# Attention B of a hybrid trunk layer: results of blocks 1 to 3 kept as [d, rows], in place of a turn back and a second transpose

## What is computed

```python
def _mixer_b(q, k, v, q_idx, k_idx, w_idx, rel_bias_b):     # 8 heads of 64, one shared k and v
    def block(args):                                         # 128 queries at a time
        ...
        _, idx = lax.top_k(score, n_sel)                     # 256 of the admissible keys
        ...
        logits = jnp.einsum('bqhd,bqkd->bqhk', qb, k_sel).astype(jnp.float32) * (B_HEAD_DIM ** -0.5)
        logits = logits + jnp.transpose(bias, (0, 1, 3, 2)).astype(jnp.float32)
        logits = jnp.where(valid[:, :, None, :], logits, NEG)
        p = jax.nn.softmax(logits, axis=-1)
        return jnp.einsum('bqhk,bqkd->bqhd', p.astype(v_sel.dtype), v_sel)
...
    merged = (jax.nn.sigmoid(gate_a) * jnp.einsum('bse,ed->bsd', o_a, w_branch_a[layer])
              + jax.nn.sigmoid(gate_b) * jnp.einsum('bse,ed->bsd', o_b, w_branch_b[layer]))
```

## Time and profile before

| | us |
|---|---|
| runs, median (lowest to highest) | 3290.53 (3290.22 to 3292.28) |
| profiled execution, device time | 3296.36 |
| its span in the profile | 3294.5 |
| TensorE busy | 3218.5 (98%) |
| VectorE, GpSimd, ScalarE busy | 1930.1, 1819.1, 1443.8 |

### The profile page before, as it was taken

One profiled execution on the slowest core, in us unless ns is written; L12 is line 12 of the kernel. 1 busy time (PEld: TensorE's weight loads), 2 busy tenths in 40 slices (PEclk: granted clock), 3 DMA queues, 4 the chain that ended last, 5 costly groups with the idle time before them and its releaser, 6 DMA issues.

```text
span 3294.5 us, 43302 instructions
## 1 busy us (share of the span) xinstructions
PE 3218.5 (98%) x15976; PEld 2696.8 (82%) x15976; DVE 1930.1 (59%) x3494; ACT 1443.8 (44%) x2610; POOL 1819.1 (55%) x1261
## 2 busy tenths in 40 slices
PE   8999999999999999999999999999999999999998
PEld 6888878878788888888888888888888789888887
DVE  3236747648565656567666766767868778621112
ACT  3324435435454534345454534736655367420001
POOL 4555554454456666655666664166666721566665
PEclk9999999999999999999999999999999999999999
DMA  5745454355524333323433332063333400333332
GB/s 159 209 138 172 115 165 138 104 153 155 190 67 155 112 106 104 116 93 112 167 106 108 96 119 93 1 233 100 96 103 115 160 15 1 137 118 98 96 103 96
DMA packets 446561, 388.98 MB, mean 118 GB/s; under 512 B 20976, under 2 KB 376560, under 8 KB 445712
## 3 DMA queue, kind: packets, MB, share of 16 engines
q1 hardware_dynamic: 424912, 341.99, 34.0%
q10 hardware_dynamic: 21440, 44.22, 3.6%
...
## 4 chain that ended last, share of the span: by engine, by line
PE 85%; DVE 6%; ACT 4%; issue 2%; POOL 1%; DMA 1%; ACTq 0%; SPq 0%; DVEq 0%; POOLq 0%
PE BANK L913 19%; PE BANK L914 19%; PE BANK L915 19%; PE LP L913 3%; PE LP L915 3%; PE LP L914 3%; PE BANK L1138 3%; PE LP L1122 2%; PE BANK L1153 2%; PE LP L1123 2%; PE LP L1023 2%; PE LP L1022 2%; PE BANK L1155 2%; PE BANK L1164 1%; ACT PThi L1445 1%
## 5 line engine op out<-in xcount | busy, mean ns | idle before, releaser
L863 POOL TENSOR_TENSOR WLO<-WRAW,WHI 128x1024 fp32r<-128x1024 f32 x456 | 1114.5, 2444 | 38.1
L861 POOL TENSOR_SCALAR WHI<-WRAW 128x1024 fp32r<-128x1024 f32 x456 | 508.1, 1114 | 1026.0 <-PE BANK L915 845.8
L913 PE MATMUL BANK<-H2hi,WHI 128*128 128x512 f32 x1376 | 542.0, 394 | 4.7 <-POOL WLO L863 4.7
L914 PE MATMUL BANK<-H2lo,WHI 128*128 128x512 f32 x1376 | 537.1, 390 | 0.0
L915 PE MATMUL BANK<-H2hi,WLO 128*128 128x512 f32 x1376 | 536.6, 390 | 0.0
L913 PE MATMUL BANK<-HThi,WHI 128*128 128x512 f32 (+1 forms) x1024 | 404.1, 395 | 2.0 <-DVE QS L1782 2.0
L914 PE MATMUL BANK<-HTlo,WHI 128*128 128x512 f32 (+1 forms) x1024 | 400.0, 391 | 0.0
L915 PE MATMUL BANK<-HThi,WLO 128*128 128x512 f32 (+1 forms) x1024 | 399.8, 390 | 0.0
L1515 ACT ACTIVATE MASK<-SCD,THR 128x896 bf16<-128x896 f32 (+5 forms) x186 | 282.0, 1517 | 243.7 <-DVE THR L1842 215.5
L913 PEld LDWEIGHTS BANK<-H2hi,WHI 128*128 128x128 f32 x1376 | 259.0, 188 | 57.2 <-issue 6.7
L915 PEld LDWEIGHTS BANK<-H2hi,WLO 128*128 128x128 f32 x1376 | 258.8, 188 | 55.2
...
## 6 DMA issues: line engine op xcount, KB each, us to landing
...
```

Source lines behind the costliest of these rows:

```text
L861: nc.gpsimd.tensor_scalar(hi, raw, 1.0, 1.0, ALU.mult, ALU.mult).then_inc(w_hi, 1)
L863: nc.gpsimd.tensor_tensor(lo, raw, hi.bitcast(f32), ALU.subtract).then_inc(w_split, 1)
L913: nc.tensor.matmul(dst, whi, mhi, start=first, stop=False)
L914: nc.tensor.matmul(dst, whi, mlo, start=False, stop=False)
```

## The change

In blocks 1 to 3 the results stay as [d, rows]; block 0 is left as it was.

- TensorE: no `turn_back`, no `out_transposes`, and `branch(b, 0, 0)` without a tail. BANK[0] of the last quad is given back by VectorE's fold.
- SP, for each quad q: `hand_sums` writes the inverted sums RS (128 rows x 4 heads) to a DRAM tensor as [heads, rows], in pieces of 4 bytes; `shift_halves` moves from XV, with four DMAs, the half that stands in other partitions than it is wanted to XZ and the other to OTB; `load_sums` reads the sums back with two DMAs, repeated over 64 partitions each, to RR. Quads 0 to 6 stand ahead of the wait for the gates, but quad 6's load of sums and quad 7's sums behind the gates' loads.
- GpSimd: `fold(q)` for quads 0 to 6, at nine groups behind the quad's end: XZ + OTB, then times RR into OTB.
- VectorE: no `scale_heads`. `invert` moves ahead, from two groups behind the quad's end to 0, 2 or 3 groups behind the first group of the quad's second pair; `whole_sums` one group ahead of it. The last quad is folded by VectorE (`fold_last`): ScalarE copies only the lo half, VectorE adds twice from PSUM and multiplies once.
- ScalarE: no `out_copy`. `split_head` waits for GpSimd's fold of quad 6 (heads of g = 0) and for `fold_last` (g = 1).

```diff
--- before.py
+++ after.py
@@ -172,6 +172,8 @@
+        XZ = [at(f"XZ{i}", [P, 2, P], f32, r3 + 28672 + 1024 * i) for i in range(2)]
+        RR = [at(f"RR{i}", [P, 2, P], f32, r3 + 30720 + 1024 * i) for i in range(2)]
...
@@ -422,6 +427,15 @@
 
         def due(times, i):
             return sum(t == i for t in times)
+
+        LASTQ = PAIRS // 2 - 1
+
+        def sums_at(b, kind, q):
+
+            if b == 0:
+                return quad_end(b, kind, q) + 2
+            count = len(groups(b, kind, 2 * q + 1))
+            return first_at(b, kind, 2 * q + 1) + (3 if count > 6 else 2 if count > 4 else 0)
 
         FIRST = -9
         AFTER = 10
@@ -659,6 +673,40 @@
                 load_table(0, TABA, tab_in, 0)
                 load_table(1, TABB, tabb_in, 0)
 
+            def hand_sums(b, q):
+
+                j, g = q // 2, q % 2
+                sp.wait_ge(inverted, n(inverted, (b, "b", q)))
+                made(sum_out[q % 2], (b, q), 16)
+                sp.dma_start(io["rsd"][b, j, 4 * g:4 * g + 4, :].rearrange("h r -> r h"), RS[:, j, 4 * g:4 * g + 4],
+                             allow_slow_non_contiguous=True).then_inc(sum_out[q % 2], 16)
+
+            def load_sums(b, q):
+
+                j, g = q // 2, q % 2
+                sp.wait_ge(sum_out[q % 2], n(sum_out[q % 2], (b, q)))
+                if q >= 2:
+                    sp.wait_ge(o_scaled, n(o_scaled, (b, q - 2)))
+                made(sum_in[q % 2], (b, q), 32)
+                for s in range(2):
+                    sp.dma_start(RR[q % 2][s * HD:(s + 1) * HD, :, :],
+                                 io["rsd"][b, j, 4 * g:4 * g + 4, :].rearrange("(e s) r -> s e r", s=2)[s].partition_broadcast(HD)
+                                 ).then_inc(sum_in[q % 2], 16)
+
+            def shift_halves(b, q):
+
+                sp.wait_ge(x_copied, n(x_copied, (b, "b", q)))
+                if q >= 2:
+                    sp.wait_ge(o_scaled, n(o_scaled, (b, q - 2)))
+                made(x_shifted[q % 2], (b, q), 64)
+                j, g = q // 2, q % 2
+                for s in range(2):
+                    own, other = (XV[q % 2][i * HD:(i + 1) * HD, :, :].rearrange("d (e s) r -> d e s r", s=2)[:, :, s, :]
+                                  for i in (s, 1 - s))
+                    r = slice(s * HD, (s + 1) * HD)
+                    sp.dma_start(XZ[q % 2][r, :, :], other).then_inc(x_shifted[q % 2], 16)
+                    sp.dma_start(OTB[r, 2 * g:2 * g + 2, j * P:(j + 1) * P], own).then_inc(x_shifted[q % 2], 16)
+
             def first_attention(t):
 
                 if t == 22:
@@ -710,12 +758,21 @@
                 b = key[2] if key[0] == "fd" else key[1]
                 LAST = PARTS[-1][0]
                 if key == ("br", b, 1, 1):
+                    for q in range(LASTQ) if b else ():
+                        hand_sums(b, q)
+                        shift_halves(b, q)
+                        if q < LASTQ - 1:
+                            load_sums(b, q)
                     last = units(b, "b")[-1]
                     sp.wait_ge(masked, n(masked, (last, chunks_of(last)[-1][0])))
                     for m in range(2):
                         for s in range(2):
                             made(gate_first[m][s], b, 16)
                             sp.dma_start(GL[:, m, s, :], io["gates"][b, s * KT + m]).then_inc(gate_first[m][s], 16)
+                    if b:
+                        load_sums(b, LASTQ - 1)
+                        hand_sums(b, LASTQ)
+                        load_sums(b, LASTQ)
                 if b + 1 < NB:
                     if key[0] == "br" and (key[3] == 0 and key[2] > 1 or key[2:] == (KT - 1, 1)):
                         sp.wait_ge(bank_full, n(bank_full, ("br", b, 0, 0)))
@@ -806,6 +863,16 @@
                     nc.gpsimd.tensor_tensor(OTlo[0][:, e, :], OTA[:, e, :], OThi[0][:, e, :].bitcast(f32), ALU.subtract
                                             ).then_inc(os_ready[0], made(os_ready[0], (b, e)))
 
+                def fold(q):
+
+                    j, g, s = q // 2, q % 2, q % 2
+                    pool.wait_ge(x_shifted[s], n(x_shifted[s], (b, q)))
+                    o = OTB[:, 2 * g:2 * g + 2, j * P:(j + 1) * P]
+                    nc.gpsimd.tensor_tensor(XZ[s][:, :, :], XZ[s][:, :, :], o, ALU.add).then_inc(o_added, made(o_added, (b, q)))
+                    pool.wait_ge(o_added, n(o_added, (b, q)))
+                    pool.wait_ge(sum_in[s], n(sum_in[s], (b, q)))
+                    nc.gpsimd.tensor_tensor(o, XZ[s][:, :, :], RR[s][:, :, :], ALU.mult).then_inc(o_scaled, made(o_scaled, (b, q)))
+
                 lowered = [0]
                 lower_times = []
                 for i, u in enumerate(units(b, "b")):
@@ -831,7 +898,7 @@
                     nc.gpsimd.tensor_tensor(FOLD[:, :], IDENT[:, 0:HD], IDENT[:, HD:P], ALU.add).then_inc(fold_set, 1)
                 for i in range(FIRST, len(all_groups(b)) + AFTER):
                     for kind, q in quads(b):
-                        if i == quad_end(b, kind, q):
+                        if i == (sums_at(b, kind, q) - 1 if b else quad_end(b, kind, q)):
                             whole_sums(kind, q)
                     for u in range(PAIRS // 2):
                         if b == 0 and i == first_at(b, "a", 2 * u + 1) - 6:
@@ -847,6 +914,9 @@
                         if lowered[0] == len(lower_times):
                             split(first_job)
                             split(first_job + 1)
+                    for q in range(LASTQ) if b else ():
+                        if i == min(quad_end(b, "b", q) + 9, quad_end(b, "b", LASTQ) + 4):
+                            fold(q)
                     if 0 <= i - end_at(b, "b", free) - 2 < ET:
                         split_low(i - end_at(b, "b", free) - 2)
 
@@ -1142,7 +1212,8 @@
                     key = (b, kind, p, g)
                     tiles, first = key_tiles(b, kind, p // 4)
                     if g == 0 and p % 2 == 0:
-                        values.bank = take("values", x_copied, (b, kind, p // 2), ("v", b, kind, p // 2))
+                        kept = (o_folded, b) if b and p // 2 == LASTQ else (x_copied, (b, kind, p // 2))
+                        values.bank = take("values", *kept, ("v", b, kind, p // 2))
                         if kind == "b" and p == 0:
                             pe.wait_ge(vb_in, n(vb_in, b))
                     dst = values.bank[:, p % 2 * 2 * P:(p % 2 + 1) * 2 * P]
@@ -1188,7 +1259,7 @@
                         next(scores)
                     if i >= 0:
                         values(*seq[i])
-                    for kind, q in quads(b):
+                    for kind, q in quads(b) if b == 0 else ():
                         if i == quad_end(b, kind, q) + 1:
                             turn_back(kind, q)
                         if q % 2 and i == quad_end(b, kind, q) + 5:
@@ -1200,7 +1271,7 @@
                     if s == 4:
                         out_transposes("b", JT - 1)
 
-                branch(b, 0, 0, tail)
+                branch(b, 0, 0, None if b else tail)
 
             def near(b, part_no, h):
 
@@ -1419,8 +1490,14 @@
 
                 def x_copy(kind, q):
                     act.wait_ge(values_done, n(values_done, last_group(b, kind, 2 * q + 1)))
-                    if quads(b).index((kind, q)) >= 2:
+                    if b and q >= 2:
+                        act.wait_ge(o_added, n(o_added, (b, q - 2)))
+                    elif b == 0 and quads(b).index((kind, q)) >= 2:
                         act.wait_ge(trans_full, n(trans_full, ("x", b) + quads(b)[quads(b).index((kind, q)) - 2]))
+                    if b and q == LASTQ:
+                        nc.scalar.copy(XV[q % 2][0:HD, :, :], in_tiles(BANK[0])[HD:P, :, :]
+                                       ).then_inc(x_copied, made(x_copied, (b, kind, q)))
+                        return
                     nc.scalar.copy(XV[q % 2][:, :, :].rearrange("p h q -> p (h q)"), BANK[0][:, :]
                                    ).then_inc(x_copied, made(x_copied, (b, kind, q)))
 
@@ -1443,7 +1520,7 @@
                         if i >= 3:
                             act.wait_ge(values_done, n(values_done, (b,) + seq[i - 3]))
                         nc.scalar.copy(PThi[r][:, 0:w, :], trans(key)[:, 0:w, :]).then_inc(pt_hi, made(pt_hi, key))
-                    for q in range(1, PAIRS // 2, 2):
+                    for q in range(1, PAIRS // 2, 2) if b == 0 else ():
                         for kind in kinds(b):
                             if i == quad_end(b, kind, q) + 8:
                                 out_copy(kind, q // 2)
@@ -1636,8 +1713,13 @@
 
                 for _ in ahead[0]:
                     pass
-                act.wait_ge(ot_ready, n(ot_ready, (b, "b", JT - 1)))
+                if b == 0:
+                    act.wait_ge(ot_ready, n(ot_ready, (b, "b", JT - 1)))
                 for e in range(ET):
+                    if b and e == 0:
```

(24 more changed lines are left out.)

3 lines of the change are left out of this document (added).

## The result

The changed kernel took 3308.06 us in the median (3302.5 to 3319.7), the kernel before beside it 3290.38 (3289.9 to 3292.3): a ratio of 1.0051, 95% interval 1.0037 to 1.0065. It is slower by 0.5%, where 3267.5 us was forecast and the range ended at 3282. The profiled execution took 3306.5 us, its span 3304.6.

What follows compares the result with a forecast made beforehand. TensorE was taken as the bound, VectorE close behind, block 2 partly latency. Savings 21.6 + 1.4 + 0.6 + 0.6 - 0.1 = 24, less 1 for block 2's loop, gave 23 us and 3267.5 us; range 3258 to 3282.

Steps and rivals of the forecast that it cites:

- The write of the sums: SP's write of inverse sums in 4-byte pieces: unknown price, taken to land in 3.3 us, with 8.7 as an end.
- Rival 2: The sums' write lands in 8.7 us, not 3.3; 14 us come back in the tails: 3282 us, chance 0.10.
- Taken away, in the middle: TensorE's turn-backs and output transposes in blocks 1 to 3: 7.2 us a block, 21.6 us in all.
- rival 1: Block 2 and places where VectorE or ScalarE are close keep their pace; half of 21.6 us lost: 3278, chance 0.18.
- the chain's shares: The chain of waits gave turn-backs 5.8, 5.1 and 5.9 us of the three stages, cited as agreeing with the removal.
- Tails: First branch jobs: the old 1.8 us loss all goes; new waits leave gains of -0.1, 0.6, 0.6 us (blocks 1, 2, 3).
- Added in the middle: Seven GpSimd folds a block at 1.45 us each, with SP's moves, all beside TensorE: priced at nothing.
- Rival 4: GpSimd becomes the gate: late shifts hold folds, then negmax and exponentials; 30 us and up, 3298 us, chance 0.08.
- SP: Seven issues a quad, 3.0 us, on an idle SP with nothing queued behind them until the gates: no cost.
- Block 3's wait of about 1 us of VectorE for GpSimd's sum: Block 3's tail: VectorE's moved inversion waits for GpSimd's last whole_sums, so values end some 1.0 us late.

Runs made afterwards that it cites:

- a2_row_write: The changed kernel with the same bytes of inverse sums written in 128 pieces of 16 bytes, not 512 of 4 (loads read a wrong order): 3280.0 us, ratio 0.9962.
- a0: The changed kernel run again, unaltered, as the base for its neighbours: 3311.7 us, ratio 1.0056 to the kernel before.
- b0_before: The kernel before, unchanged, as a control with a trace of its own: 3293.5 us, ratio 1.0004.
- b1: The changed kernel with only what it removes, no DMA of sums or halves and no GpSimd folds: 3273.8 us, ratio 0.9947 to the kernel before.

## Why the prediction was wrong, step by step

**The write of the sums: the step that failed.** I took 3.3 us from loads of 4-byte pieces and kept 8.7 as an end; 7.6 to 9.5 us it was. The row was of another kind: loads at the start of the kernel, which read small pieces from memory and don't write them to it. Rival 2 named the mechanism, with a chance of 0.10. The rule behind it (the Trainium skill, DMA: Bandwidth & Descriptors, Rules for kernel authors: one descriptor per element, rearrange it) is borne out here: the profile has 528 packets for the write, and 512 pieces in place of 128 cost 31.7 us.

**Rival 2's price of 14 us was half of the truth.** It had the delay of the three tails (5.4 + 5.4 + 3.4) and missed three things. After a stall of 4.4 to 8.3 us TensorE ran at a granted clock of 0.50 for some 5 us, up to 2.4 us more in each tail. In block 1 the last write also started late, 5.0 us behind its inversion, as SP was behind. And there the sums of the quads before came late as well, with GpSimd standing in front of the negations: 6 us. Tails +9.1, +7.1 and +8.1 over a2_row_write and 6.1 us in block 1's middle are 30.4 us, against 31.7 measured between a0 and a2.

**Taken away, in the middle.** The removed time was sized right (7.16 of 7.2 us a block), its worth was not: 12.8 of 21.6 us between b0_before and b1, 14.4 between before and b1. This is the second term that was mis-sized. It is rival 1's mechanism, which I had put at 0.18; it works in block 3 as well, where 5.2 to 5.7 of 7.2 us came, though TensorE was busy 30.00 of 30 us in the earlier trace rows. I argued against it with the chain's shares, but the chain tells what TensorE did then, not what would be late next.

**Tails.** "All of it goes": right, 14.2 to 12.3 us in b1_removals. What I put in its place left gains of -0.1, 0.6 and 0.6 us (blocks 1, 2, 3); with a write that lands early, a2_row_write, they are 0.2, 0.4 and 1.9. The whole kernel with the removals alone gains 12.8 + 5.7 = 18.5 us, and measured 17.3 (3291.1 to 3273.8).

**Added in the middle.** Folds at 1.45 us a pair (0.74 each), hidden: right, a2 has b1's middles. Rival 4 had the right place, GpSimd in front of the negations, but what came late was the sums, not the shifts, and only in block 1, where a quad is shortest.

**SP.** That "nothing is queued behind them until the gates" was wrong: behind each write stand SP's own next quad and, in the tail, the loads. The issues cost 0.61 us each, not 0.43, which by itself cost nothing that any run shows.

**Block 3's wait of about 1 us of VectorE for GpSimd's sum** is there: 1.23 us before 2829.84. It comes before the first branch matmul, so it counts in the middle and not in the tail.

**In all** the forecast missed a0_after's 3311.7 by 44.2 us. The write is 31.7 of them, and the middles some 9 (22.0 forecast, 13.0 between b0_before and a2_row_write); the kernel before, 1.8 us slower beside a0_after than beside the forecast, and the noise between traces take up the rest.
